# The last expert's tail: when the reads of the scattered sums are issued, in a diffusion trunk layer with 16 experts

## The reference

```python
def expert_choice_ffn(h, w_router, w_gate, w_up, w_down):
    ...
    g, idx = lax.top_k(aff.T, cap)
    xe = xt[idx]
    hid = jax.nn.silu(jnp.einsum('ecd,edf->ecf', xe, w_gate)) * jnp.einsum('ecd,edf->ecf', xe, w_up)
    ye = jnp.einsum('ecf,efd->ecd', hid, w_down) * g[..., None].astype(h.dtype)
    out = jnp.zeros_like(xt).at[idx.reshape(-1)].add(ye.reshape(-1, D))
    return out.reshape(B, S, D)
...
    y = expert_choice_ffn(h, w_router, w_gate, w_up, w_down)
    x = x + gt2 * rmsnorm(y, g_post_ffn)
```

## Time and profile before

| What | us |
|---|---|
| median of 3 runs | 1947.46 |
| the three runs | 1947.1, 1947.46, 1952.33 |
| the profiled execution | 1953.02 |
| its span, first to last instruction | 1951.2 |
| PE busy in it | 1910.8 (98%) |
| DVE, ACT, POOL busy | 459.4, 301.4, 144.7 |
| HBM traffic | 642 MB, 329 GB/s over the span |

### The profile page before, as it was taken

The page is one execution under the profiler, slowest core; times in us unless marked ns, Lnnn a source line. Parts: engine busy times, 40 slices in busy tenths (PEclk is TensorE's granted clock), DMA queues, the critical chain, the costliest instruction groups (busy, mean ns, idle before and its releaser), DMA issues.

```text
span 1951.2 us, 36708 instructions
## 1 busy us (share of the span) xinstructions
PE 1910.8 (98%) x16641; PEld 888.6 (46%) x16641; DVE 459.4 (24%) x825; ACT 301.4 (15%) x548; POOL 144.7 (7%) x216
## 2 busy tenths in 40 slices
PE   6999999999979999999999999999999999999997
PEld 3889787779853333323333333333333333333322
DVE  3432355557352101111010111101111110110114
ACT  4222245444220000000000000000000000000001
POOL 1000000000121101001010100101010010100004
PEclk9999999999979999999999999999999999999999
DMA  8851111112569999999999999999999999999997
GB/s 350 336 198 63 46 50 55 44 53 88 233 262 366 412 420 413 418 414 419 413 412 420 413 418 414 419 414 413 420 412 417 414 418 407 413 414 413 418 400 290
DMA packets 101412, 644.51 MB, mean 330 GB/s; under 512 B 11760, under 2 KB 14208, under 8 KB 43408
## 3 DMA queue, kind: packets, MB, share of 16 engines
q1 hardware_dynamic: 93792, 618.23, 77.5%
q0 software_dynamic: 6608, 20.85, 3.4%
q10 hardware_dynamic: 864, 3.15, 0.4%
HBM read 625.66 MB, written 16.52 MB: 329 GB/s over the span
## 4 chain that ended last, share of the span: by engine, by line
PE 96%; DVE 1%; DMA 1%; POOL 1%; issue 0%; ACT 0%; SPq 0%; POOLq 0%; DVEq 0%; ACTq 0%
PE ps L892 94%; PE ps L1073 1%; DMA out<-fin 1%; DMA x<-in_x_sample 0%; PE ps L995 0%; PE ps L1210 0%; PE ps L900 0%; PE ps L929 0%; DVE Gs L1921 0%; POOL rsx L733 0%; DVE topi L2095 0%; POOL rsx L732 0%; DVE topv L2094 0%; PE ps L1103 0%; DVE work L2097 0%
## 5 line engine op out<-in xcount | busy, mean ns | idle before, releaser
L892 PE MATMUL ps<-ring,xeT 128*32 128x512 f32 (+1 forms) x9216 | 914.4, 557 | 0.0
L892 PEld LDWEIGHTS ps<-ring,xeT 128*32 128x32 f32 x9216 | 296.9, 110 | 609.8 <-issue 608.5
L892 PE MATMUL ps<-ring,hidT 128*32 128x512 f32 x4224 | 459.6, 592 | 3.1 <-DMA ring<-in_w_dn 3.1
L892 PEld LDWEIGHTS ps<-ring,hidT 128*32 128x32 f32 x4224 | 136.1, 110 | 317.4 <-issue 310.8
L2233 DVE TENSOR_TENSOR hid<-sil,ps 128x768 f32<-128x768 f32 (+1 forms) x48 | 42.6, 887 | 915.1 <-ACT sil L1708 915.1
L1708 ACT ACTIVATE sil<-ps 128x768 f32<-128x768 f32 (+1 forms) x48 | 36.4, 758 | 959.9 <-PE ps L892 959.9
L892 PE MATMUL ps<-hT_hi,gq_hi 128*128 128x320 f32 x256 | 88.1, 344 | 0.0
L892 PE MATMUL ps<-in_hi,hT_hi 128*128 128x384 f32 x240 | 82.2, 343 | 0.0
L892 PE MATMUL ps<-in_lo,hT_hi 128*128 128x384 f32 x240 | 80.4, 335 | 0.0
L892 PE MATMUL ps<-in_hi,hT_lo 128*128 128x384 f32 x240 | 80.3, 335 | 0.0
L892 PE MATMUL ps<-hT_hi,gq_lo 128*128 128x320 f32 x256 | 79.1, 309 | 0.0
(11 more groups left out here) (262 smaller groups left out, 1432.0 us busy)
## 6 DMA issues: line engine op xcount, KB each, us to landing
ring<-in_w_gu SPq DMA_DIRECT2D x256, 1024.0 KB, 27.1
ring<-in_w_dn SPq DMA_DIRECT2D x176, 1024.0 KB, 24.1
ring<-in_w_gu_rest SPq DMA_DIRECT2D x128, 768.0 KB, 24.1
slab_y<-in_w_mod_blocks SPq DMA_DIRECT2D x8, 2048.0 KB, 8.9
in_slab<-in_w_in_blocks SPq DMA_DIRECT2D x6, 1536.0 KB, 8.7
gq<-in_w_gates SPq DMA_DIRECT2D x16, 512.0 KB, 3.4
slab<-in_w_mod_blocks SPq DMA_DIRECT2D x3, 2048.0 KB, 16.3
x<-in_x_sample SPq DMA_DIRECT2D x8, 512.0 KB, 6.4
```

The costliest lines, as they stand in the source:

```text
L892: return pe.matmul(out, lhsT, rhs, start=first, stop=last, **kw)
```

## The change

The reads of tiles 0 and 1 stay where they were. Squares 0 and 1 and silu of group 2 come next, then a wait for the landing of the fourth last transfer of weights, and behind it the reads of tiles 2, 3 and 4 and the gains' read. The wait `xs_ready` goes with the squares. No other engine's list changes, and what is computed stays the same.

```diff
--- before.py
+++ after.py
@@ -1745,17 +1745,24 @@
             silu(last, 0)
             silu(last, 1)
             act.wait_ge(scattered, 16 * NT + 16 * (E_ - 1))
-            for t in LAST:
+            def sums_rows(t):
                 act.wait_ge(w_used, FREE + t // 2)
                 act.dma_start(fin[t][:, :], ysum_dram[t * P:(t + 1) * P, :]).then_inc(ld_x[t], 16)
+
+            for t in LAST[:2]:
+                sums_rows(t)
+            act.wait_ge(xs_ready, E_)
+            for i in range(2):
+                tokens_square(i)
+            silu(last, 2)
+            late = len(FLOW_W) - 4
+            act.wait_ge(w_ld[late % RS], 16 * (late // RS + 1))
+            for t in LAST[2:]:
+                sums_rows(t)
             act.wait_ge(gg_loaded, 16)
             act.wait_ge(w_used, FREE + 3)
             rows = gg_dram[KD:2 * KD, :].rearrange("(o k) p -> o (k p)", o=1)
             act.dma_start(gg_c[:, :], rows.to_broadcast([P, D])).then_inc(gg_loaded, 16)
-            act.wait_ge(xs_ready, E_)
-            for i in range(2):
-                tokens_square(i)
-            silu(last, 2)
             for i in range(2, NT):
                 tokens_square(i)
             act.wait_ge(ctx_summed, 1)
```

## The result

The changed kernel took 1959.76 us (median of 4 runs, 1959.26 to 1961.18), the kernel before 1949.55 us beside it (4 runs, 1947.1 to 1952.33). The ratio is 1.0049, with a 95% interval of 1.003 to 1.0068: slower, by 5.8 to 13 us. The profiled execution took 1959.26 us with a span of 1957.5 us, 6.3 us more than the span of before, although it came to the last expert's second group 1.2 us earlier.

What follows compares the result with a forecast made beforehand. PE, busy 98% of the span, bounds the kernel; late reads would make DVE set the end. yrB +7.0 less 0.5 gives +6.5 us on the 1947.46 median: 1954.0 us, range 1948.5 to 1959.5.

Steps and rivals of the forecast that it cites:

- Step 1: Weights on the slower half of the DMA engines: fourth last transfer lands 4.9 us earlier, ending ACT's new wait at 1924.8.
- Step 2: First late read on ACT's queue: tile 2 lands 8.25 us after issue, at 1933.0, its first packet moving after 4.5 us.
- Step 3: PE's last weights: land at about 1933.6, all three gaps go, and PE stops 3.1 us earlier, at 1940.1.
- Step 4: Late tiles through ACT, POOL and DVE: landings at 1933.0, 1935.7 and 1938.1, tile 4 done at 1943.65.
- Step 5: End of DVE's queue: yrB starts at 1945.3, 7.0 us later; 0.5 us comes back after it, so +6.5 us.
- the 1.63 us: Wait of the context's scatters on POOL for the prompt's store, claimed to be no longer needed.
- two ends of before: In the kernel before, PE's end (1943.27) and the tile chain's last store (1943.20) were claimed 0.07 us apart.
- DVE's saved wait for PE: Ahead of yrA on DVE: 0.73 us of waiting for PE would go, of which 0.5 us was taken back.
- A: Late reads come quickly through idle DMA capacity, tile 2 in at 1928.0: +1.5 us, 1949.0 us; chance 0.17.
- B: PE still sets the end, tiles done in time, so the kernel ends 3.1 us sooner: 1944.3 us; chance 0.03.
- C: Slower half serves ACT's reads only after the last weights, or gain row slow: +8 to +9.5, 1956.2 us; chance 0.13.
- D: New wait on ACT has no effect, weights landing before it; reads go 2.6 us sooner: +4, 1951.4 us; chance 0.12.

Runs made afterwards that it cites:

- e10: Changed kernel, no edit, executed a third time: 1959.08 us against 1951.0 for the kernel before, ratio 1.0041.
- e4: Changed kernel without the three late tile reads, the gains' read and the wait, so outputs are wrong: span 1945.2 us, tail 52.12 us.
- e6: Changed kernel with the wait on the last transfer of weights in place of the fourth last: span 1962.7 us, tail 67.06 us.
- e8: Kernel before with only the gains' read moved, behind squares 2 to 4 and the wait for the fourth last transfer: span 1948.6 us, tail 57.86 us.
- e5: Kernel before, no edit, executed again: 1952.21 us against 1949.66 for the identical kernel, ratio 1.001.
- e1: Changed kernel, no edit, executed again: 1956.56 us against 1947.58 for the kernel before, ratio 1.0049.
- e2: Changed kernel without the wait for the fourth last transfer of weights, order kept: span 1951.3 us, tail 61.41 us.
- e3: Changed kernel with all tile reads early again, only the gains' read and squares 2 to 4 behind the wait: span 1954.2 us, tail 58.97 us.
- e7: Changed kernel with DVE's half rows of the latents' gains moved ahead of finish(2): span 1956.4 us, tail 61.64 us.
- e9: Changed kernel with the gains' read back in its early place, the three tile reads still late: span 1954.1 us, tail 64.32 us.

## Why the prediction was right, and where it was off

The forecast was +6.5 us, through the tail; the tails of three traces of after and two of before differ by 62.92, 62.92 and 64.50 against 55.42 and 55.97, on average 7.8 us.

Step 1, the wait ends at 1924.8, 29.0 us after the mark: measured 28.5, 28.6 and 30.3. Right, with a scatter that I had not allowed for.

Step 2, a read takes 8.25 us there: 8.03, 7.91 and 8.30. Right, by the likeness to the first read of before, and not by its working: I let the first packet move only 4.5 us after the issue. The DMA view of after, from 1923 to 1926 us and from 1926 to 1930 (queue: packets, MB, share; the issue was at 1923.11):

```profile
q1 hardware_dynamic: 74, 0.55, 44.2%
q10 hardware_dynamic: 67, 0.26, 32.3%
```

```profile
q10 hardware_dynamic: 286, 1.05, 65.3%
q1 hardware_dynamic: 75, 0.53, 32.4%
```

Within 2.9 us of the issue 67 packets were through, and half of the 2 MB in the next four. The landings of the shares show why the tile is late all the same: of tile 2's 16 shares 8 had landed 3.2 to 3.5 us after the issue, the other 8 came after 7.0 to 8.0. The last weights are split alike: 8 of their shares landed between 1914.4 and 1915.8, long before the issue, and 8 between 1929.2 and 1933.5. That it is the same half of the engines both times fits, but the landings don't name the engine.

Step 3, all gaps on PE go: it failed. One gap of 1.26 us stayed (2.48 in e10), and PE stopped 2.3 us sooner, not 3.1. The last three transfers took 10.46 us from the end of the wait (1923.11 to 1933.57) instead of 7.38 + 1.4, 1.7 us more than forecast. With no reads beside them, in e4 and e6, they took 7.8 us by their landings, so 0.4 us of it is the weights' own pace; the rest is the term that was too small, what the reads take from the weights, some 2.6 us instead of 1.4, as their packets move at once and not after 4.5 us. It cost nothing, since PE is not on the path.

Step 4: tiles at 1933.0, 1935.7 and 1938.1 were forecast, 37.2, 39.9 and 42.3 us after the mark; measured 36.6, 40.0 and 42.5. yrB 7.0 us later was forecast, 7.04 measured in after (8.7 in e10). Right.

Step 5: here the size was off. From yrB's start to the end it took 13.36 us in after and 12.90 in before: 0.46 us more, where I took 0.5 off. The reason lies on POOL (its timeline in after; the earlier trace rows answer to it):

```profile
1947.14 0.54 POOL L872 TENSOR_TENSOR rsz<-rsz,mhalf 64x1 f32<-64x1 f32 x1 [7.26 <-DVE rsz L2319]
1949.31 1.35 POOL L881 DMA_INDIRECT out<-yrB,idx_oB  x1 [1.62 <-DVE yrB L2324]
1950.96 0.84 POOL L881 DMA_INDIRECT out<-yrB,idx_oB  x1 [0.30 <-issue]
1951.83 0.58 POOL L872 TENSOR_TENSOR rsz<-rsz,mhalf 128x1 f32<-128x1 f32 x1
```

The first scatter begins 0.86 us after yrB is done (1948.45), when the prompt's store has long landed (1945.1). In before yrB was done at 1942.62 and the scatter began at 1943.47, 0.85 us later: the same. So the 1.63 us that the earlier trace rows put down to the store were not its wait, and I was wrong to take them as released; in e4 and e8, too, the scatter begins 0.85 us after yrB. The store of the earlier trace rows only happened to land then (in e5 as well, where the scatter began 0.87 us after yrB). That also takes back my sentence that two ends of before stood 0.07 us apart: only PE's did count.

There was no 0.5 us to take back in the first place. In before, too, POOL's last power came right behind the second scatter (POOL's timeline of before, further down than the earlier trace rows):

```profile
1944.72 0.84 POOL L881 DMA_INDIRECT out<-yrB,idx_oB  x1 [0.30 <-issue]
1945.59 0.58 POOL L872 TENSOR_TENSOR rsz<-rsz,mhalf 128x1 f32<-128x1 f32 x1
```

The second scatter ends at 1945.56, the power starts at 1945.59. So the path from yrB to the end leads over POOL's two scatters in both kernels, and DVE's saved wait for PE can't show. Nearly all of the 0.46 us comes from the first of them: it takes 1.35 us instead of 0.94 wherever DVE goes from yrB straight on to yrA (after, e1, e2, e3, e6, e7, e9, e10), and 0.94 where DVE first waits for PE (before, e5, e4, e8). No run shows why.

**Numbers.** 1954.0 was forecast and 1959.76 measured, 0.3 us over the top of my range (1959.5). By the ratio, on the median that the forecast started from, it is 1947.46 x 1.0049 = 1957.0, inside the range and 3.0 over the forecast. 1.3 us of the difference is the tail's, by the traces, of which 1.0 is step 5 (0.46 lost, 0.5 taken off). Most of the rest is what the part ahead of the tail takes, whose end, the mark, lies anywhere from 1889.8 to 1895.8 in the twelve traces, whichever kernel it is: the runs of after lie between 1954.68 and 1962.13, those of before mostly at 1946.4 to 1948 or at 1949.6 to 1952.8, a few up to 1955.2. That the forecast's 6.5 us are so near the 7.8 of the tails is in part luck, as step 2 had the right time with a wrong account of when the reads begin to move. The lowest of each, 1954.68 and 1946.43, differ by 8.3 us. The ratios, 1.0049, 1.0049 and 1.0041, stand for 8 to 9.6 us; their intervals reach down to 5 to 7 us and hold the 7.8 of the tails. Whether the last 1 to 2 us are scatter, or something ahead of the tail that the few traces didn't catch, stays open.

**Rivals.** A (quick reads) fell to the reads of 8 us; even with no weights left one takes 4.73 (e6, with two stores still queued). The Trainium skill's fit (DMA: Bandwidth & Descriptors, Anatomy of one DMA), made on the GpSimd path, gives an estimate of 3.2 us for 512 KB. Neither read agrees with it as a whole; the half of tile 2's shares that landed after 3.2 to 3.5 us does. B fell because DVE was late. C's mechanism, reads served only behind the weights, is not what happens (tile 2's last share landed at 1931.1, the last weights at 1933.5), though the size (+8 and more) was met in e10. D fell: silu was over 2.1 us before the wait was.

None of the kernels that compute the right outputs has a shorter tail than before. The room is the 3.1 us of PE's gaps, and every read that was moved here landed after DVE needed it. Putting the last expert's sums ahead of late tiles on DVE was not tried, and neither was a place for a read between the old one (up to 12.3 us after the mark) and the one behind silu of group 2 (26 us).

## What to carry to other kernels

A transfer that is off the path can still not be put off freely: ask when its last share lands under the load of that moment (8 us here for 512 KB), what is queued in order behind its consumer, and how much idle time that queue has (3.92 us here). Freeing the busiest engine of a 3 us wait is worth nothing if the engine that takes its results comes 7 us later. And where a run scatters by more than the effect, compare traces from a mark behind the common part.

## What the runs showed of the hardware that I had not expected

- Moving a single read of 512 KB behind the fourth last weights (e3, e8) did not let the last weights land any sooner: 41.6 us after the mark, against 41.3 and 41.75 with all reads early.
- In both of these PE's last piece took 7.91 us instead of 6.21. The granted clock fell from full speed (2.4 GHz) to half (1.2 GHz) for 3.4 us of that piece, after waits of PE of 1.68 and 2.03 us in e8 (1.64 and 2.03 in e3) with one short piece of matmuls between them. PE's timeline and windows of e8:

```profile
1929.29 1.07 PE L892 MATMUL ps<-ring,hidT 128*32 128x512 f32 x8 [1.68 <-DMA ring<-in_w_dn]
1932.38 7.91 PE L892 MATMUL ps<-ring,hidT 128*32 128x512 f32 x56 [2.03 <-DMA ring<-in_w_dn]
```

```profile
1927.00:1929.00 2.00, 0.61 (x8) 0.00 (x0) 0.00 (x0) 0.00 (x0) 0.00 (x0) 1.00 0.64 266
1929.00:1932.00 3.00, 1.07 (x8) 0.16 (x8) 0.57 (x1) 0.00 (x0) 0.00 (x0) 1.00 0.50 205
1932.00:1936.00 4.00, 3.62 (x24) 1.01 (x28) 3.87 (x7) 0.60 (x1) 0.00 (x0) 0.65 0.67 269
```

  Single waits of 2.36 (e9) and 2.48 us (e10) in the same place left the clock at full speed, and so did the three shorter ones of before.
- The same program reaches its last expert up to 5.8 us sooner or later (after, e1 and e10), and the stretches of low clock between 541 and 577 us differ in length with it: 20.5, 10.2 and 23.9 us.
